# A residual with tokens on the partitions: output and down products with the activations stationary, norms tile by tile inside them, modulation on TensorE

## The chip, the cores and the metric

The kernel runs on one core of a Trainium2 chip. The metric is device time in microseconds (us) from the start to the end of one execution, as the median of several; the profile adds one execution with the time of every instruction. The engines are named as the profile names them: PE is TensorE (matmuls; PEld its weight loads), DVE is VectorE, ACT is ScalarE, POOL is GpSimd, and SP is the engine that issues nearly all DMAs. PE's clock has two levels, and "granted clock" 1.00 is the higher one, 2.4 GHz, 0.50 the lower.

## What is computed

Two layers of a diffusion backbone over 512 latent tokens and 256 context tokens, with 1024 features. Each sub-layer norms x, shifts and scales it, runs a mixer or the feed-forward part, norms the result, multiplies it by a gate and adds it to x. Shift, scale and gate come from a conditioning vector times a matrix of 1024 x 6144 per layer ("modulation"), and differ for latent and context tokens.

```python
for l in range(DEPTH):
    need_ctx = l < DEPTH - 1
    mod = jnp.split((silu_c @ ada_w[l] + ada_b[l])[:, None, :], 6, axis=-1)
    ...
    h = modulate(rms_norm(x, mix_pre_g[l]), mod[0], mod[1])
    ...
    x = x + mod[2] * rms_norm(y, mix_post_g[l])
    h = modulate(rms_norm(x, ffn_pre_g[l]), mod[3], mod[4])
    x = x + mod[5] * rms_norm(conv_ffn(h, ffn_w_in[l], ffn_conv_w[l], ffn_w_out[l]), ffn_post_g[l])
```

Layer 0's mixer is a convolution of width 31 beside a bidirectional mLSTM of four heads; layer 1's is a pooling group beside attention with six query heads. Both have one input and one output projection. `conv_ffn` is up product (gate and value, 2 x 2816 columns), a convolution of width 3 on the gate, silu, product and down product. In layer 1 only the latent tokens go on behind the mixer's keys and values.

## The kernel before

**Number format and products.** Every large product is three matmuls: both factors are split into a high part (`_hi`, the fp32r format) and a low part (`_lo`, the rest), and hi x hi, hi x lo and lo x hi are added in PSUM. `product` (matmul in L463) keeps 128 x 128 of weights stationary and moves 512 tokens and then 256 (only 512 in most of layer 1). A unit is 256 output features over all 1024 input features: 48 matmuls of 512 columns and 48 of 256.

**Weights** come in granules of 512 KB, two a unit. SP loads one to `raw` (two places), ACT makes `w_hi` (L855), DVE makes `w_lo` (L1247), and these have four places. The counters `low`, `high`, `unit_done` and `set_free` order all that: SP may load a granule when the one two before has its low part, and ACT may overwrite a `w_hi` when PE is done with its unit. PSUM `acc` has two sets, which the units take in turn; `set_free` gives one back. Each engine runs its instructions in the order in which its block writes them, and waits at a semaphore hold up all that stands behind them on that engine.

**Residual and norms.** The residual `xT` and the mixer's result `y` have features on the partitions, so a norm over features is a sum over partitions. It is a stage of its own between products: ACT squares 128 features of all tokens at a time (L880 for x, L891 for y), PE sums them by matmuls with a column of ones (`column_sums`, L498), DVE and ACT make the inverse root, PE spreads it over the partitions (`spread`, L510), and DVE and ACT do the residual (L1363), the normed and modulated value (L1344, ACT L903) and its low part (L1336). Matmuls without use (`keep_clock`, L518) run where PE would stand still in a norm. At the start x is loaded with tokens on the partitions, squared (L937) and transposed, and at the end `xT` is transposed back (L489), copied (L1239) and stored.

**Modulation.** The matrix comes in chunks of 256 columns, 1 MB each. DVE multiplies a chunk by the conditioning vectors and adds it up (L1259, L1266), PE sums that over the partitions inside a unit (L476), and ACT takes it (L869). The first eight chunks are shared by PE (L585) and DVE at the start, 8 to 11 lie in the even layer's input products, 12 to 19 in its output product, and the others in layer 0's feed-forward part.

**The order of stages.** Input products (`conv`, `gate`, `qkov`), the convolution's taps on DVE (L1474, `conv_done` after them, L1520), mLSTM, `out0`, two norms, then three groups of up and down products (`up00`, `down00`, ... `down02`, with 8, 8 and 6 tiles of 128 hidden features each), a norm of y and one of x, layer 1's `in1`, `kin`, `vin`, attention, `out1`, norms and `up10` to `down12`. The mLSTM goes through a list of items: "S" is a piece of scores (PE L699, ACT and DVE L1568 make `probs` of it), `weigh` multiplies probabilities by values (PE L672), "X" is the transposition of a head's result; the pieces of the convolution's norm (L641, L650) lie in the first head. The first half of out0's first unit stands in PE's queue ahead of the last head's transposition. DVE then merges a head with its gate, ACT and POOL (L1859) split it in `h_hi` and `h_lo`.

## Time and profile before

| | |
|---|---|
| median of 3 runs | 1904.1 us (1900.16 to 1906.55) |
| the profiled execution, its span | 1905.9 us |
| PE busy, weight loads | 1771.0 us (93%), 1501.2 us (79%) |
| DVE, ACT, POOL busy | 1149.3, 558.5 and 32.6 us |
| moved by DMA | 157.8 MB, 83 GB/s on average |

"Busy" counts all time in which an engine executes: matmuls that only keep the clock up count too. The chain of work that ended last tells, step by step back from the end, what each instruction waited for; the windows tell how busy each engine was in a stretch of the program.

### The profile page before, as it was taken

How to read it: one execution, taken by the hardware profiler on the slowest of the kernel's cores; microseconds unless marked ns; L12 is line 12 of the kernel's file. 1: busy time of each engine (PE TensorE's matmuls, PEld its weight loads, DVE VectorE, ACT ScalarE, POOL GpSimd, SP SyncE). 2: the span in 40 equal slices, each digit the busy share in tenths (PEclk: the TensorE clock that was granted, in tenths of full speed). 3: DMA queues.
4: the chain of work that ended last, by engine and by line, in shares of the span. 5: the costliest groups of instructions: out<-in, count | busy, mean ns of one | idle time of the engine just before them, and what ended most of it. 6: DMA issues, size and time to landing. Idle time of an engine off the chain costs nothing.

```text
span 1905.9 us, 25175 instructions
## 1 busy us (share of the span) xinstructions
PE 1771.0 (93%) x9614; PEld 1501.2 (79%) x9614; DVE 1149.3 (60%) x1899; ACT 558.5 (29%) x786; POOL 32.6 (2%) x68
## 2 busy tenths in 40 slices
PE   5899996777998999999999999999899999999997
PEld 3688875556897888888888888887587878888885
DVE  4787986455856776676755764542884555344344
ACT  3323222652123332123212222231232343222232
POOL 0000000220000000000000000000000000000000
PEclk9899996798987999999999999798999899999997
DMA  8232200012411334433332421040002033233321
GB/s 293 67 89 90 66 25 33 17 39 89 139 61 45 99 121 132 133 100 121 124 119 67 132 74 59 1 135 23 0 1 74 16 110 99 85 103 97 93 81 61
DMA packets 156405, 157.80 MB, mean 83 GB/s; under 512 B 9442, under 2 KB 153506, under 8 KB 156330
## 3 DMA queue, kind: packets, MB, share of 16 engines
q1 hardware_dynamic: 155760, 156.55, 25.8%
q8 instruction: 50, 0.82, 0.2%
q10 hardware_dynamic: 570, 0.22, 0.0%
q14 instruction: 25, 0.20, 0.0%
HBM read 154.63 MB, written 2.12 MB: 82 GB/s over the span
## 4 chain that ended last, share of the span: by engine, by line
PE 79%; DVE 13%; ACT 3%; DMA 2%; issue 2%; POOL 0%; ACTq 0%; SPq 0%; DVEq 0%
PE acc L463 60%; PE acc L518 3%; PE acc L498 3%; DVE conv_u L1474 3%; PE acc L829 2%; PE acc L476 2%; PE acc L808 2%; PE acc L672 1%; DVE tbuf L1344 1%; PE acc L489 1%; DVE h_lo L1336 1%; DVE ada_acc L1266 1%; DVE w_lo L1247 1%; PE acc L650 1%; PE acc L510 1%
## 5 line engine op out<-in xcount | busy, mean ns | idle before, releaser
L463 PE MATMUL acc<-h_hi,w_hi 128*128 128x512 f32 x1744 | 520.0, 357 | 18.4 <-DVE h_lo L1336 8.3
L463 PE MATMUL acc<-h_hi,w_lo 128*128 128x512 f32 x1744 | 516.9, 355 | 0.0
L463 PE MATMUL acc<-h_lo,w_hi 128*128 128x512 f32 x1744 | 515.3, 354 | 0.0
L463 PEld LDWEIGHTS acc<-h_hi,w_hi 128*128 128x128 f32 x1744 | 287.9, 191 | 69.4 <-issue 9.0
L463 PEld LDWEIGHTS acc<-h_lo,w_hi 128*128 128x128 f32 x1744 | 286.2, 191 | 47.1
L463 PEld LDWEIGHTS acc<-h_hi,w_lo 128*128 128x128 f32 x1744 | 286.2, 190 | 46.8
L1247 DVE TENSOR_TENSOR w_lo<-raw,w_hi 128x1024 fp32r<-128x1024 f32 x190 | 225.7, 1224 | 90.3 <-ACT w_hi L855 89.8
L855 ACT ACTIVATE w_hi<-raw 128x1024 fp32r<-128x1024 f32 x190 | 193.2, 1053 | 186.8 <-PE acc L463 97.5
L1266 DVE SCALAR_TENSOR_TENSOR ada_acc<-ada_w,cond,ada_acc 128x256 f32<-128x256 f32 x476 | 194.3, 479 | 1.6
L463 PE MATMUL acc<-hid_hi,w_hi 128*128 128x512 f32 (+1 forms) x528 | 160.1, 358 | 0.0
L463 PE MATMUL acc<-hid_lo,w_hi 128*128 128x512 f32 (+1 forms) x528 | 159.5, 356 | 0.0
L463 PE MATMUL acc<-hid_hi,w_lo 128*128 128x512 f32 (+1 forms) x528 | 159.4, 356 | 0.0
L1474 DVE SCALAR_TENSOR_TENSOR conv_u<-conv_u,dw_w 128x783 f32<-128x783 f32 x120 | 124.1, 1034 | 4.0
L869 ACT ACTIVATE mods<-acc,vec 128x2 f32 (+1 forms) x80 | 17.4, 262 | 363.3 <-PE acc L476 363.0
L1655 DVE TENSOR_SCALAR hid<-gpad,ffn_cw 128x512 f32 x66 | 25.2, 438 | 128.2 <-ACT gpad L1122 128.2
L463 PEld LDWEIGHTS acc<-hid_lo,w_hi 128*128 128x128 f32 x528 | 86.8, 188 | 15.5
L463 PEld LDWEIGHTS acc<-hid_hi,w_lo 128*128 128x128 f32 x528 | 86.7, 188 | 15.4
L463 PEld LDWEIGHTS acc<-hid_hi,w_hi 128*128 128x128 f32 x528 | 86.7, 188 | 15.0
L1247 DVE TENSOR_TENSOR y<-acc,y 128x1536 f32 (+5 forms) x18 | 24.0, 1342 | 89.9 <-PE acc L463 78.8
L1653 DVE SCALAR_TENSOR_TENSOR hid<-gpad,ffn_cw,hid 128x512 f32 (+1 forms) x132 | 77.6, 657 | 0.0
L518 PEld LDWEIGHTS acc<-ident,ones 128*128 128x128 f32 x528 | 70.4, 217 | 1.9 <-issue 1.0
L672 PEld LDWEIGHTS acc<-v_tok,probs 128*128 128x128 f32 x336 | 46.9, 220 | 31.2 <-DVE probs L1568 20.5
(225 smaller groups left out, 1697.9 us busy)
## 6 DMA issues: line engine op xcount, KB each, us to landing
raw<-in_ffn_w_in SPq DMA_DIRECT2D x88, 512.0 KB, 4.7
ada_w<-in_ada_w SPq DMA_DIRECT2D x80, 512.0 KB, 3.6
raw<-in_ffn_w_out SPq DMA_DIRECT2D x40, 512.0 KB, 4.5
raw<-in_even_w_in SPq DMA_DIRECT2D x24, 512.0 KB, 4.3
ada<-in_ada_w SPq DMA_DIRECT2D x8, 1024.0 KB, 12.2
raw<-in_odd_w_in SPq DMA_DIRECT2D x12, 512.0 KB, 3.6
raw<-in_even_w_out SPq DMA_DIRECT2D x8, 512.0 KB, 5.2
raw<-in_odd_w_out SPq DMA_DIRECT2D x8, 512.0 KB, 4.1
```

Source lines behind the costliest of these rows:

```text
L463: last = nc.tensor.matmul(acc[:, s, m, t0:t1], w[:, slot, kk, c], x[:, k, t0:t1], start=(k == 0 and q == 0), stop=(k == ktiles - 1 and q = ...
L476: last = nc.tensor.matmul(acc[:, s, 0, at_:at_ + 1], (ada_acc, second or ada_acc_b)[x][:, c, q * P:(q + 1) * P], ones[:, 0:1], start=True, ...
L498: last = nc.tensor.matmul(acc[:, s, 0, j:j + 1], src(j), ones[:, 0:1], start=(m == 0 and j == 0), stop=(m == len(sources) - 1 and j == til ...
L518: nc.tensor.matmul(acc[:, u % 2, 1, 512:512 + P], ones[:, :], ident[:, :], start=True, stop=True)
L672: last = nc.tensor.matmul(dst, probs[e % 4][:, t * P - t0:t * P - t0 + P], v_tok[:, ORDER[q], hd, :], start=(q, d, t) == FIRST_TOUCH[b], s ...
L808: last = nc.tensor.matmul(acc[:, 0, n % 2, t0:t1], inb[:, 2 + hd, i * P:(i + 1) * P], kT[:, hd // 3, t0:t1], start=True, stop=True)
L829: last = nc.tensor.matmul(acc[:, 1, 1, c:c + P], v1[:, j, (hd // 3) * HD:(hd // 3 + 1) * HD], pT[:, n % 2, j * P:(j + 1) * P], start=(j == ...
L855: nc.scalar.activation(w_hi[:, n % 4], raw[:, n % 2], ACT.Copy).then_inc(high, 1)
L1247: return nc.vector.tensor_tensor(out_, in0, in1, op)
L1266: ins = nc.vector.scalar_tensor_tensor(dst[:, c, :], w(k), scale, dst[:, c, :], ALU.mult, ALU.add)
L1474: ins = nc.vector.scalar_tensor_tensor(dst, src, tap, dst, ALU.mult, ALU.add)
L1653: ins = nc.vector.scalar_tensor_tensor(dst, src, c, dst, ALU.mult, ALU.add)
```

## The change

The residual `x` and `y` now have tokens on the partitions. `out0`, `out1` and the down products take 128 tokens of `h` or `hid` as the stationary operand and move 512 output columns of the weights (`token_products`, L637), in two halves of the output (`a` is 0 or 1), a half over all tiles of 128 tokens; a granule is 256 input features of 512 columns. The four products that a norm follows (`out0`, `down02`, `out1`, `down12`, "edges") do their second half tile by tile, and each tile's norm, gate, residual, next norm and transposition go on while PE does the other tiles: ACT squares with a running sum and takes roots, DVE updates x, PE transposes tile j-2 behind tile j (`turn`, L623), DVE modulates from PSUM, ACT makes `h_hi` and POOL `h_lo`. The first two units of what follows (up products or `in1`) run in segments of 256 tokens (`first_products`). The gates go as rows to DRAM and come back on all partitions. The norms' matmuls with ones, the fills and the transpositions at the end are gone, and x is stored as it is. Modulation: chunks 0 to 7 are matmuls with two moving columns at the start, 8 to 23 the same inside mLSTM (`ada_chunk`, L786, behind each "S" with q of 2 or more; the chunk is in the room of `raw`, one buffer of two halves), and layer 1's 24 chunks stay with DVE in `up00` and `up01`. The convolution's weights' low parts lie at other places on DVE, and out0 stands wholly behind the last head. The down products of layer 0 have 792 such matmuls, out0 has 288, out1 192, and layer 1's down products 528: 1800 in all.

```diff
+        def load_token(sp, name, w, first, k):
+            n, half = G[name] + k, TOK[name].half
+            a, g = divmod(k, half)
+            sp.wait_ge(low, n + 3)
+            sp.dma_start(raw[:, n % 2].rearrange("p (k a) c -> p k (a c)", k=2),
+                         w[:, first + 2 * g:first + 2 * g + 2, 512 * a:512 * a + 512]).then_inc(raw_full[n % 2], 16)
...
+            def load_ada_m(first, end):
+                for e in range(first, end):
+                    for half in range(2):
+                        if e:
+                            sp.wait_ge(adam_used, 2 * (e - 1) + half + 1)
+                        else:
+                            sp.wait_ge(low, G["out0"] + 8)
+                        sp.dma_start(ada_m[:, half], w_ada[0][:, 4 * half:4 * half + 4, (8 + e) * 256:(9 + e) * 256]
...
+                if h:
+                    load_ada_m(4 * h - 3, 4 * h + 1)
+            load_ada_m(13, 16)
+            def gate_rows(row, l, comp, streams):
+                for s in range(streams):
+                    sp.dma_start(g_dram[row + s].rearrange("(k p) -> p k", p=P), mods[:, l, comp, :, s],
+                                 allow_slow_non_contiguous=True).then_inc(gates_out, 16)
+            def gates_everywhere(row, dst, streams):
+                for s in range(streams):
+                    sp.dma_start(dst[:, s, :], g_dram[row + s].partition_broadcast(P)).then_inc(gates_in, 16)
+            sp.wait_ge(adam_used, 32)
+            load_token(sp, "out0", w_even_out, 0, 4)
+            load_token(sp, "out0", w_even_out, 0, 5)
+            sp.wait_ge(gates_set, 1)
+            gate_rows(0, 0, 2, 2)
+            gate_rows(2, 0, 5, 2)
+            sp.wait_ge(gates_out, 64)
+            gates_everywhere(0, gates[0], 2)
+            load_token(sp, "out0", w_even_out, 0, 6)
+            load_token(sp, "out0", w_even_out, 0, 7)
...
+        def first_products(pe, u, n, rhs, segs, ready, between, ada=None):
+            for e, (t0, t1) in enumerate(segs):
+                for x in range(2):
+                    s = (u + x) % 2
...
+                        if not x and not part:
+                            ready(e)
+                        for kk in range(4):
+                            k = 4 * part + kk
+                            for m in range(2):
+                                c = slice(m * P, (m + 1) * P)
+                                for q, (w, x_) in enumerate(((w_hi, rhs[0]), (w_hi, rhs[1]), (w_lo, rhs[0]))):
+                                    last = nc.tensor.matmul(acc[:, s, m, t0:t1], w[:, m_ % 4, kk, c], x_[:, k, t0:t1],
+                                                            start=(k == 0 and q == 0), stop=(k == KD - 1 and q == 2))
+                    if e == len(segs) - 1:
+                        if ada:
+                            last = ada_columns(pe, u + x, 0, ada[x])
+                    between(2 * e + x)
+        def turn(pe, name, j):
+            q = TOK[name].chain + j
+            pe.wait_ge(xn_ready, NT + q + 1)
+            if j >= 2:
+                pe.wait_ge(t_ready, KD + q - 1)
+            for k in range(KD):
+                last = nc.tensor.transpose(turned_bank(name, j, k), xn[j % 2][:, k * P:(k + 1) * P], ident[:, :])
+            last.then_inc(turned, 1)
...
+        def token_products(pe, name, lhs, ready):
+            def step(a, g, j):
+                m_ = n + a * half + g
+                for kk in range(2):
+                    k = 2 * g + kk
+                    for q, (w, x_) in enumerate(((w_hi, lhs[0]), (w_lo, lhs[0]), (w_hi, lhs[1]))):
+                        last = nc.tensor.matmul(tile_bank(name, a, j), x_[:, k, j * P:(j + 1) * P],
+                                                w[:, m_ % 4, 2 * kk:2 * kk + 2, :].rearrange("p a c -> p (a c)"),
+                                                start=(k == 0 and q == 0), stop=(k == 2 * half - 1 and q == 2))
+                return last
+            psum_free(pe, d)
+            for a in range(2):
+                if a and t.edge:
+                    for j in range(nt):
+                        if j >= 2:
+                            pe.wait_ge(tile_free, t.tiles + (j - 2 if j < 4 else nt + j - 2) + 1)
+                        for g in range(half):
+                            if not j:
+                                pe.wait_ge(low, n + half + g + 5)
+                            last = step(1, g, j)
+                            if j == nt - 1 and g < half - 1:
+                                last.then_inc(part_used, 1)
+                        last.then_inc(unit_done if j == nt - 1 else tile_full, 1)
+                        if name != "down12" and j >= 2:
+                            turn(pe, name, j - 2)
+                    continue
+                for g in range(half):
+                    pe.wait_ge(low, n + a * half + g + 5)
+                    ready(2 * g)
+                    ready(2 * g + 1)
+                    for j in range(nt):
+                        if not g and not a and j == 4 or not g and a and not j:
+                            psum_read(pe, d - 1)
+                        if not g and a and j >= 2:
+                            pe.wait_ge(tile_free, t.tiles + j - 1)
+                        last = step(a, g, j)
...
-            def norm_x(u, norm, tokens, diag_count):
-                psum_free(pe, u)
-                keep_clock(u, 70 * tokens // T)
-                column_sums(u, [lambda j, m=m: sq[:, m % 2, j * P:(j + 1) * P] for m in range(KD)], tokens // P,
-                            lambda m: pe.wait_ge(sq_ready, KD * norm + m + 1), sq_used)
-                keep_clock(u, 6)
-                spread(u + 1, diag, tokens, diag_count)
-                keep_clock(u + 1, 12)
...
+            def ada_chunk(e):
+                for q in range(2):
+                    c = 944 + 4 * e + 2 * q
+                    for k in range(KD):
+                        if not q and k % 4 == 0:
+                            pe.wait_ge(adam_full[k // 4], 16 * (e + 1))
+                        last = nc.tensor.matmul(acc[:, 0, 1, c:c + 2], ada_m[:, k // 4, k % 4, q * P:(q + 1) * P], cond[:, k, :],
+                                                start=False, stop=(k == KD - 1), skip_group_check=True)
+                        if q and k % 4 == 3:
+                            last.then_inc(adam_used, 1)
...
-                if z == len(ITEMS) - 1:
-                    assert U["out0"] % 2 == 0
-                    pe.wait_ge(sem("sums_read"), HEADS)
-                    product(pe, U["out0"], G["out0"], h, h_tiles(1), parts=(0,))
...
+                if kind == "S" and q >= 2:
+                    ada_chunk(chunk)
+                    chunk += 1
...
+            def x_squares(j, q):
+                nc.scalar.activation(xn[j % 2][:, :], x[:, j, :], ACT.Square, scale=1.0 / 32, accum_out=xsq[:, j:j + 1]
+                                     ).then_inc(sem("x_square"), 1)
+                act.wait_ge(sem("x_square"), q + 1)
+                nc.scalar.activation(xroot[:, 0, j:j + 1], xsq[:, j:j + 1], ACT.Sqrt, bias=eps[:, 0:1]).then_inc(x_root, 1)
+            def x_normed(j, q):
+                act.wait_ge(x_scale, q + 1)
+                nc.scalar.activation(xn[j % 2][:, :], x[:, j, :], ACT.Copy, scale=xroot[:, 1, j:j + 1]).then_inc(xn_ready, 1)
+            def tile_high(name, j):
+                act.wait_ge(t_ready, KD + TOK[name].chain + j + 1)
+                nc.scalar.activation(h_hi[:, :, j * P:(j + 1) * P], tb[j % 2][:, :, :], ACT.Copy).then_inc(t_high, 1)
...
+                    y_squares(name, 1, j)
+                    q = t.chain + j
+                    act.wait_ge(y_square, t.squares + nt + j + 1)
+                    nc.scalar.activation(yroot[:, 0, j:j + 1], ysq[:, j, 1:2], ACT.Sqrt, bias=ysq[:, j, 0:1]).then_inc(y_root, 1)
+                    if not on:
+                        continue
+                    if j >= 3:
+                        tile_high(name, j - 3)
+                    act.wait_ge(x_new, q + 1)
+                    if j >= 2:
+                        act.wait_ge(turned, q - 1)
+                    x_squares(j, NT + q)
+                    x_normed(j, NT + q)
...
+            def modulated(name, j, l, comp, tiles):
+                for k in tiles:
+                    last = nc.vector.tensor_scalar(tb[j % 2][:, k, :], turned_bank(name, j, k), mods[:, l, comp + 1, k, s_:s_ + 1],
+                                                   mods[:, l, comp, k, s_:s_ + 1], ALU.mult, ALU.add)
...
+                    summed(name, 2, 1, j)
+                    q = t.chain + j
+                    if on and j >= 2:
+                        modulated(name, j - 2, l, comp, range(0, 4))
+                    dve.wait_ge(y_root, q + 1)
+                    sd.done(nc.vector.reciprocal(yroot[:, 1, j:j + 1], yroot[:, 0, j:j + 1]))
+                    if not mixer:
+                        dve.wait_ge(y_gated, t.sums // 2 + j + 1)
+                    sd.wait()
+                    nc.vector.scalar_tensor_tensor(x[:, j, :], y[:, j, :], yroot[:, 1, j:j + 1], x[:, j, :], ALU.mult, ALU.add
+                                                   ).then_inc(x_new, 1)
+                    if not on:
+                        continue
+                    if j >= 2:
+                        modulated(name, j - 2, l, comp, range(4, 8))
+                    x_scales(j, NT + q)
+                for m in range(2, half) if on else ():
+                    take_low(n + half + m + 4)
+                for j in range(nt - 2, nt) if on else ():
+                    modulated(name, j, l, comp, range(8))
...
+                def tile_low(j):
+                    pool.wait_ge(t_high, KD + t.chain + j + 1)
+                    c = slice(j * P, (j + 1) * P)
+                    nc.gpsimd.tensor_tensor(h_lo[:, :, c], tb[j % 2][:, :, :], h_hi[:, :, c].bitcast(F32), ALU.subtract
+                                            ).then_inc(h_tile, 1)
+                for j in range(t.nt):
+                    if name[:3] != "out":
+                        pool.wait_ge(y_square, t.squares + t.nt + j + 1)
+                        nc.gpsimd.tensor_tensor(y[:, j, 512:1024], y[:, j, 512:1024],
+                                                gates[EDGES.index(name)][:, stream(j), 512:1024], ALU.mult).then_inc(y_gated, 1)
+                    if j >= 3 and name != "down12":
+                        tile_low(j - 3)
+                for j in range(t.nt - 3, t.nt) if name != "down12" else ():
+                    tile_low(j)
```

PE inside mLSTM, in the second half of a head, before (`qkov` is the scores' operand, `probs_72` and `probs_77` are probabilities, `h_tok` a head's result):

```order
L699 MATMUL acc<-qkov 128x512
L672 MATMUL acc<-v_tok,probs_72 128x129 x9
L672 MATMUL acc<-v_tok,probs_77 128x129 x2
L672 MATMUL acc<-v_tok,probs_72 128x129 x5
L489 MATMUL acc<-ident,h_tok 128x128 x6
L699 MATMUL acc<-qkov 128x512 x2
L672 MATMUL acc<-v_tok,probs_72 128x129 x3
L672 MATMUL acc<-v_tok,probs_77 128x129 x2
L699 MATMUL acc<-qkov 128x512
L672 MATMUL acc<-v_tok,probs_72 128x129 x5
L699 MATMUL acc<-qkov 128x512
```

and after, the same place (`ada_m` is a chunk of the modulation):

```order
L807 MATMUL acc<-qkov 128x512
L786 MATMUL acc<-cond,ada_m 128x2 x16
L774 MATMUL acc<-v_tok,probs_70 128x129 x9
L774 MATMUL acc<-v_tok,probs_75 128x129 x2
L774 MATMUL acc<-v_tok,probs_70 128x129 x5
L680 MATMUL acc<-ident,h_tok 128x128 x6
L807 MATMUL acc<-qkov 128x512
L786 MATMUL acc<-cond,ada_m 128x2 x16
L807 MATMUL acc<-qkov 128x512
L786 MATMUL acc<-cond,ada_m 128x2 x16
L774 MATMUL acc<-v_tok,probs_70 128x129 x3
L774 MATMUL acc<-v_tok,probs_75 128x129 x2
```

Behind each piece of scores there are 16 matmuls with two columns; between the first chunk of a head and the second 22 other matmuls and a score stand, between the second and the third one score.

PE between the last unit of out0 and the first up product, before (`ones` with `sumsq` and `sq` are the norms' sums, `ident,ones` fills):

```order
L476 MATMUL acc<-ones,ada_acc 128x1 x4
L476 MATMUL acc<-ones,ada_acc_b 128x1 x4
L518 MATMUL acc<-ident,ones 128x128 x6
L498 MATMUL acc<-ones,sumsq 128x1 x6
L498 MATMUL acc<-ones,sq 128x1 x12
L510 MATMUL acc<-diag,ones 128x512
L510 MATMUL acc<-diag,ones 128x256
L518 MATMUL acc<-ident,ones 128x128 x70
L498 MATMUL acc<-ones,sq 128x1 x48
L518 MATMUL acc<-ident,ones 128x128 x6
L510 MATMUL acc<-diag,ones 128x512
L510 MATMUL acc<-diag,ones 128x256
```

and after, inside out0's second half (`xn_87` is a normed tile of x):

```order
L637 MATMUL acc<-w_hi,h_hi 128x512
L637 MATMUL acc<-w_lo,h_hi 128x512
L637 MATMUL acc<-w_hi,h_lo 128x512
L623 MATMUL acc<-ident,xn_87 128x128 x8
L637 MATMUL acc<-w_hi,h_hi 128x512
L637 MATMUL acc<-w_lo,h_hi 128x512
L637 MATMUL acc<-w_hi,h_lo 128x512
```

The sums, spreads and fills are gone, and eight transposes of a tile lie between the products of two others.

ACT in the edge of out0, after (`junk` takes the squares of y, `xn` those of x and then the normed x, `tb_89` is a modulated tile); before, a norm stood alone in its queue:

```order
L1016 ACTIVATE junk_92,small<-acc 128x512
L1046 ACTIVATE small<-small 128x1
L1003 ACTIVATE h_hi<-tb_89 128x8x128
L990 ACTIVATE xn_88,small<-x 128x1024
L993 ACTIVATE small<-small 128x1
L998 ACTIVATE xn_88<-x,small 128x1024
L1016 ACTIVATE junk_91,small<-acc 128x512
L1046 ACTIVATE small<-small 128x1
L1003 ACTIVATE h_hi<-tb_90 128x8x128
```

A tile's squares, roots and normed x now stand in one queue with an older tile's `h_hi`, so the next tile's square waits for all of them.

## Rows read from the trace of the kernel before

**Rows 1.** The profile's page, first line and first part: busy us, share, instructions:

```profile
span 1905.9 us, 25175 instructions
PE 1771.0 (93%) x9614; PEld 1501.2 (79%) x9614; DVE 1149.3 (60%) x1899; ACT 558.5 (29%) x786; POOL 32.6 (2%) x68
```

**Rows 2.** The page's fourth part, shares of the chain that ended last:

```profile
PE 79%; DVE 13%; ACT 3%; DMA 2%; issue 2%; POOL 0%; ACTq 0%; SPq 0%; DVEq 0%
```

**Rows 3.** Windows by stage, one row each; columns as its first row says:

```profile
core 0: us, PE busy (x) PEld busy (x) DVE busy (x) ACT busy (x) POOL busy (x), PEclk, DMA share, GB/s
0.00:79.80 79.80, 51.53 (x268) 35.11 (x268) 41.08 (x96) 31.09 (x51) 3.83 (x7) 0.94 0.58 188
279.10:308.40 29.30, 9.36 (x54) 6.89 (x52) 28.30 (x30) 12.06 (x16) 1.03 (x2) 0.61 0.15 54
308.40:318.80 10.40, 10.38 (x49) 10.39 (x49) 1.71 (x4) 0.40 (x1) 0.29 (x1) 0.50 0.01 2
318.80:431.30 112.50, 87.12 (x471) 67.12 (x470) 52.71 (x123) 64.77 (x140) 25.60 (x57) 0.86 0.07 24
...
1293.10:1436.80 143.70, 129.59 (x773) 100.56 (x771) 95.93 (x167) 41.11 (x70) 0.00 (x0) 0.92 0.03 8
...
1878.90:1905.90 27.00, 14.52 (x70) 9.91 (x69) 12.56 (x22) 6.59 (x8) 0.00 (x0) 0.64 0.20 78
```

**Rows 4.** The chain in order of time: start us, us, engine, line, instructions:

```profile
98.55 1.68 PE acc L476 x16
...
541.99 17.08 PE acc L518 x140
559.07 17.53 PE acc L498 x96
...
631.99 16.76 PE acc L463 x96
...
1313.43 17.54 PE acc L783 x144
...
1526.86 352.03 PE acc L463 x1536
```

**Rows 5.** Groups by form: busy us, mean ns of one, idle us before, releaser:

```profile
L1266 DVE SCALAR_TENSOR_TENSOR ada_acc<-ada_w,cond,ada_acc 128x256 f32<-128x256 f32 x476 | 194.3, 479 | 1.6
L672 PE MATMUL acc<-v_tok,probs 128*128 128x129 f32 x336 | 49.9, 309 | 21.7 <-DVE probs L1568 21.7
L1363 DVE SCALAR_TENSOR_TENSOR xT<-y,mods,xT 128x512 f32<-128x512 f32 x32 | 23.6, 744 | 0.0
L1859 POOL TENSOR_TENSOR h_lo<-merged,h_hi 128x768 fp32r<-128x768 f32 x4 | 7.4, 1848 | 29.3 <-ACT h_hi L1063 29.3
L937 ACT ACTIVATE xsq_junk<-x_tok 128x1024 f32<-128x1024 f32 x6 | 6.4, 1061 | 0.1
```

**Rows 6.** Waits by pair: us in total, times, longest us:

```profile
PE acc L650 <- DVE mark L1520: 14.0, 1, 14.0
```

**Rows 7.** DMA issues: count, KB each, median us to landing:

```profile
ada_w<-in_ada_w SPq DMA_DIRECT2D x80, 512.0 KB, 3.6
...
raw<-in_even_w_in SPq DMA_DIRECT2D x8, 8.0 KB, 2.0
```

**Rows 8.** The timeline at several places: start us, us, engine, instruction:

```profile
93.84 2.35 DVE L1247 TENSOR_TENSOR w_lo<-raw,w_hi 128x1024 fp32r<-128x1024 f32 x2
...
444.94 0.82 PE L489 MATMUL acc<-ident,h_tok 128*128 128x128 f32 x6
...
447.78 1.87 POOL L1859 TENSOR_TENSOR h_lo<-merged,h_hi 128x768 fp32r<-128x768 f32 x1 [18.79 <-ACT h_hi L1063]
...
448.68 3.19 DVE L1247 TENSOR_TENSOR w_lo<-raw,w_hi 128x1024 fp32r<-128x1024 f32 x2 [1.61 <-ACT w_hi L855]
...
1900.47 1.94 ACT L1239 ACTIVATE o_tok<-acc 128x1024 f32<-128x1024 f32 x2 [1.18 <-PE acc L489]
```

1058 lines of the change are left out of this document (501 added, 557 removed).

## The prediction, made before the changed kernel ran

> **What bounds the kernel now.** I read the page first: of 1905.9 us TensorE (PE) is busy 93% [rows 1], and 79% of the chain that ended last is its work [rows 2]. But busy is not useful. The windows by stage [rows 3] show where PE works for nothing or waits: 28.3 us idle before the second unit of products, 20 us idle in the tail of the convolution (279.1 to 308.4, DVE busy 28.3 of 29.3), then column sums at a granted clock of 0.50 of full speed, and 12.5 us idle at the end. The chain in order of time [rows 4] shows what the norms between stages cost: in one norm of x, 17.1 us of matmuls L518 that only keep the clock up, and 17.5 us of column sums L498. Elsewhere PE runs product after product without a gap: a unit of 48 matmuls of 512 columns and 48 of 256 takes 16.76 us, and 1536 matmuls of 512 columns take 352.03, which is 0.2292 us each. With activations stationary and 256 columns moving (the value projection, L783), 144 take 17.54, 0.1218 each. So the form that the change introduces is there already, at half the width, and costs per column what the old one does.
>
> **Start to the first column sums of the convolution: -26.4.** Before, these sums end at 318.8 [rows 3]. The change takes the modulation of four chunks off DVE. A chunk costs it 14 instructions of 0.48 us [rows 5] and two smaller ones, some 7.4 us, so 30 in all. PE loses the three places where it folds them (1.68 each [rows 4], 5.0) and some 3.4 of waits for w_lo behind them. The first unit of products ends 4.7 earlier by my count (74 for 78.7): chunks 0 to 7 are matmuls with two columns, x is normed tile by tile (a square of 1024, 1.06 us, and a copy of the same size each), and after that POOL makes h_lo, 8 times 1.85 [rows 5]. That is 13.1 by the last unit of qkov. PE's wait of 14.0 for the convolution's last tile [rows 6] goes, since DVE has 30 us less in front of it; what is late next is PE itself. I add 0.7 for a copy that now stands behind the last unit. 13.1 + 14.0 - 0.7 = 26.4.
>
> **mLSTM: +38.5.** Sixteen chunks of 16 two-column matmuls go into PE's queue, four a head. The nearest row is L476, 16 in 1.68 us, so 27 for all at full clock. They also wait for data: one buffer of two halves, each freed by the last matmul that reads it, and a half of 512 KB lands in 3.6 us when alone [rows 7], 5.2 as the second of two by my estimate. The queue puts some 3.5 us of other work between chunks one and two of a head (22 matmuls of 128 or 129 columns at 0.14, as six transposes take 0.82 [rows 8], and a score), 0.3 between two and three and 1 between three and four, so some 10 us of waiting a head. Queued behind are the weighing of probabilities and the next scores, for which DVE and ACT wait. PE already waits 21.7 in this stage for DVE's probabilities [rows 5], 5 a head, and that covers part. I take 4 for the first head, where the convolution's norm leaves gaps, and 11.5 for each other one: 38.5. The bounds are 28 (only the matmuls) and 50 (nothing covered).
>
> **Last weighing to the end of the second up unit: -67.2.** Before, from 431.3 [rows 3] to 631.2, which is 0.8 before the row of the next unit starts [rows 4]: 199.9 us. After: out0 stands wholly behind the last head, whose norm, transposes, merge and modulation take 11.2 before PE may start, with 2.2 for a low clock; the first 512 output columns are 144 matmuls, 33.0. Then the second half, the turns and the first two up units. PE's own work there is 33.0, six times eight transposes at 1.05 a tile (a little under six's 0.82 by four thirds), and 288 matmuls of 256 columns at 0.1218, in all 74.4. The chain of a tile is longer than PE's 6.5: square 0.8, root, reciprocal, x update 1.29 (from 0.744 for 512 columns and 0.478 for 256), square 1.25, root, reciprocal, copy 1.05, with the semaphores 6.2. From the fourth tile on POOL's h_lo of 1024 columns (2.45, from 1.85 for 768) comes between, 8.4 to 8.8. Laid out tile by tile, the last tile is ready at 66 to 71, and the second unit ends at 83.8 to 88.6. I take 86.3. 11.2 + 2.2 + 33.0 + 86.3 = 132.7. The edge needs its gate rows: four DMAs of 1024 elements. The nearest row is 512 short runs in 2.0 us [rows 7], so 16 for the four, then two broadcasts; with 33 us until DVE wants them I charge nothing, and if that cover is gone each us late costs one.
>
> **To the end of kin: -40.5.** Before, 631.2 to 1293.1, 661.9. After: 20 up units at 16.75, 14 gaps of 0.78 for the modulation's fold, and 792 matmuls of the down products at 0.2292, 527.4 in all. The edge of down02, with y from SBUF, two multiplications more and three granules a half, ends 76 to 84 us after its first half, of which 24.8 is counted; 55.3. Then two units of 11.0 and one of 16.75. Sum 621.4.
>
> **Layer 1: -6.1.** Attention (143.7 us [rows 3]) is untouched. Before, out1 starts at 1436.8 and the second up unit ends at 1537.9, 11 after the last row of [rows 4] starts; 101.1. After: 22 + 73 by the same layout with four tiles. The rest of the FFN stays, its down products in the other form at the same price.
>
> **Tail: -17.6.** Before, 27.0 us stand behind the last product [rows 3]. After, the last tile's sum 0.7, square 0.8, gate on POOL 1.25, x update 1.29 and latencies, 5.9, and 3.5 for the last store (before, the last copy ends at 1902.4 [rows 8]). Small stalls that drop the clock: +3.
>
> The sum is -116.3, from 1905.9 to 1789.6. The profiled execution was 1.8 above the median of the runs shown, so 1788.
>
> **A rule weighed.** Two w_lo on DVE took 3.19 us where POOL's h_lo ran in front and into them, and 2.35 elsewhere [rows 8]; the first did not get going before POOL was done. I costed the edges half way between a DVE that waits so for every h_lo and one that never does. The Trainium skill ("SBUF — State Buffer", section "Who interferes with whom") has it that a VectorE instruction with two SBUF inputs and a GpSimd one exclude each other for their whole length, an exclusive lock on a shared port. By the rule the sum comes to 1795; with no lock anywhere, the start's 8 us included, to 1773.
>
> **The rivals.** (1) It goes better: no lock, and chunks that wait little (28 for 38.5): 25 less, 1763. For it speaks that DMA is 0.07 busy in mLSTM [rows 3]. 17%. (2) The waits for chunks put PE's clock down through mLSTM. The stage already has 0.86 with PE idle 25 us; at 0.50 the column sums took about twice their time. 30 more: 1818. 18%. (3) The tile chain is longer than laid out (periods of 11, or gate rows late), some 12 in each of three edges: 1825. Against it speaks that every operation in it has a row. 13%. (4) The other side: the down and output products. There are 1800 matmuls with tokens stationary and 512 weight columns moving; the trace shows that form only at 256 columns. If each took over 0.293 instead of 0.2292, 64 ns more, the 116 are gone, and at 0.31 the kernel is at 1935. Against it speaks L783 [rows 4]. 3%. That the norms' matmuls are not gone can't be: the order shows no L518.
>
> **How the numbers follow.** Forecast 49%, with its own range 1765 to 1805 (the bounds of mLSTM's 28 and 50, of the edges' lock). The range reaches into (1), (2) and (3): 1740 to 1832. A change of 0.3%, about 6 us, is what a measurement can tell; (1) to (3) and the forecast are all far below, so faster 0.96, slower 0.03 from (4), same 0.01.
>
> **What would show it.** In the changed profile: L637 at 0.229 us a matmul; two stretches of L786 with a wait for ada_m of 3 to 5 us in each head, and the last weighing near 443; in out0's edge a new x every 6 us, later every 8 to 9; the first up unit beginning some 45 us after the first half; no fills; 9 us from the last matmul to the end. The prediction is wrong if PE waits over 15 us a head, if the granted clock in mLSTM is near 0.5, or if L637 is over 0.25.

## The result, and the profile after

The changed kernel takes 1941.05 us (median of 4, 1934.49 to 1943.12) against 1903.55 for the kernel before beside it. The ratio of the runs is 1.0181, 95% interval 1.0159 to 1.0204: slower by 1.6 to 2.0%, clear of the noise though not clearly over 2%, where the prediction had 1788 and gave "slower" 0.03. Its profiled execution spans 1940.8 us, 34.9 more than before.

The page of the kernel after, first and fourth part:

```profile
span 1940.8 us, 23097 instructions
PE 1771.4 (91%) x9170; PEld 1512.9 (78%) x9170; DVE 962.0 (50%) x1488; ACT 564.3 (29%) x817; POOL 100.0 (5%) x102
...
PE 74%; DVE 11%; ACT 5%; issue 4%; DMA 3%; POOL 1%; ACTq 0%; DVEq 0%; POOLq 0%; SPq 0%
PE acc L584 33%; PE acc L637 18%; PE acc L608 3%; PE acc L786 3%; PE acc L774 3%; PE acc L708 3%; DVE ada_acc L1370 2%; DVE w_lo L1351 2%; PE acc L680 2%; DMA ada_w<-in_ada_w 2%; PE acc L948 2%; DVE x L1493 2%; PE acc L927 2%; PE acc L807 1%; ACT xn L990 1%
```

PE is as busy as before to half a microsecond (1771.0 in [rows 1]), although fills and column sums are gone: something as large has come in. New in the chain are L708 and L786, the chunks of the modulation, and DVE's sums of layer 1 with their loads. The windows by stage say where (columns as in [rows 3]):

```profile
42.65:97.06 54.41, 54.41 (x258) 54.41 (x256) 11.12 (x21) 6.76 (x8) 11.72 (x6) 1.00 0.19 58
333.84:529.90 196.06, 179.44 (x983) 158.44 (x982) 53.00 (x123) 64.99 (x140) 25.80 (x57) 0.72 0.30 93
541.20:582.00 40.80, 40.76 (x169) 33.54 (x170) 9.05 (x14) 8.14 (x17) 1.83 (x1) 0.94 0.48 75
582.00:660.10 78.10, 70.94 (x464) 65.36 (x463) 47.51 (x101) 35.59 (x59) 14.63 (x6) 0.96 0.18 56
660.10:788.70 128.60, 114.29 (x633) 99.68 (x634) 89.79 (x175) 37.62 (x44) 0.00 (x0) 0.91 0.34 106
856.30:1031.10 174.80, 154.53 (x833) 134.65 (x832) 110.19 (x198) 36.72 (x58) 0.00 (x0) 0.91 0.43 135
1227.00:1303.30 76.30, 61.87 (x351) 54.67 (x350) 49.04 (x90) 36.21 (x60) 22.02 (x12) 0.87 0.10 30
1342.10:1492.40 150.30, 133.59 (x771) 104.33 (x771) 98.12 (x169) 42.16 (x70) 0.00 (x0) 0.89 0.05 15
```

Laid beside the prediction's own stages (the differences are after less before, in us; the 3 us that the prediction adds for small stalls belong to no row):

| stage | before | after | foretold | measured |
|---|---|---|---|---|
| start to the end of the first column sums of the convolution | 318.8 | 333.8 | -26.4 | +15.0 |
| mLSTM, to the last weighing | 112.5 | 196.1 | +38.5 | +83.6 |
| to the end of the second up unit | 199.9 | 130.2 | -67.2 | -69.7 |
| to the end of kin | 661.9 | 682.0 | -40.5 | +20.1 |
| attention | 143.7 | 150.3 | 0 | +6.6 |
| out1 to the start of the third up unit | 101.1 | 99.5 | -6.1 | -1.6 |
| the rest of layer 1's products | 341.0 | 340.9 | 0 | -0.1 |
| behind the last product | 27.0 | 8.0 | -17.6 | -19.0 |

The residual's part came as foretold: norms, edges, tail. Three stages miss by 41, 45 and 61 us, 147 together, of an error of 151 (1940.8 for 1789.6). In all three the modulation is computed, in the first two by two-column matmuls on PE, in the third by DVE, whose sums PE folds (adds up over the partitions, L566) inside a unit. The chain in order of time shows what a chunk costs there:

```profile
42.65 54.41 PE acc L708 x256
97.06 214.65 PE acc L584 x1200
...
398.09 3.47 PE acc L786 x32
...
460.16 4.92 DMA ada_m<-in_ada_w
465.12 5.28 PE acc L786 x24
...
583.60 1.30 DVE x L1493
589.19 1.30 DVE x L1493
596.05 1.30 DVE x L1493
602.90 2.73 DVE x L1493
...
611.19 2.72 DVE x L1493
...
671.92 1.87 PE acc L566 x8
673.79 19.40 PE acc L584 x96
```

A chunk is 16 matmuls in the program and 32 records in the trace: at best 3.47 us, 0.108 a record. At the start a record takes 0.2125 (54.41 / 256), and behind a wait for data 0.22 (5.28 / 24). The rows "DMA ada_m" are the loads from issue to landing; PE itself stands idle for less of it, here 1.80 and 0.35 us, since a score and eight records of the next chunk go on beside the load. I had taken "16 in 1.68" of [rows 4] for one chunk. The order printed ahead of the prediction has that place as 4 + 4 matmuls, so 16 records were 8 matmuls already.

### The profile page after: what moved, and what is told of

Same layout as the page of the kernel before. It is cut to its first block, busy times and chain, and to the rows that moved or that the text cites. A ratio compares the mean times of both kernels' runs of the same rounds, so it can differ in the third digit from the quotient of the medians.

```text
span 1940.8 us, 23097 instructions
## 1 busy us (share of the span) xinstructions
PE 1771.4 (91%) x9170; PEld 1512.9 (78%) x9170; DVE 962.0 (50%) x1488; ACT 564.3 (29%) x817; POOL 100.0 (5%) x102
## 4 chain that ended last, share of the span: by engine, by line
PE 74%; DVE 11%; ACT 5%; issue 4%; DMA 3%; POOL 1%; ACTq 0%; DVEq 0%; POOLq 0%; SPq 0%
PE acc L584 33%; PE acc L637 18%; PE acc L608 3%; PE acc L786 3%; PE acc L774 3%; PE acc L708 3%; DVE ada_acc L1370 2%; DVE w_lo L1351 2%; PE acc L680 2%; DMA ada_w<-in_ada_w 2%; PE acc L948 2%; DVE x L1493 2%; PE acc L927 2%; PE acc L807 1%; ACT xn L990 1%
## 5 line engine op out<-in xcount | busy, mean ns | idle before, releaser
L584 PE MATMUL acc<-h_hi,w_hi 128*128 128x512 f32 (+1 forms) x1424 | 420.4, 357 | 1.7 <-DVE w_lo L1351 1.7
L584 PE MATMUL acc<-h_lo,w_hi 128*128 128x512 f32 (+1 forms) x1424 | 420.6, 357 | 0.0
L584 PE MATMUL acc<-h_hi,w_lo 128*128 128x512 f32 (+1 forms) x1424 | 418.9, 356 | 0.0
L584 PEld LDWEIGHTS acc<-h_hi,w_hi 128*128 128x128 f32 x1424 | 235.3, 193 | 40.8 <-DVE w_lo L1351 1.9
L637 PE MATMUL acc<-w_hi,hid_hi 128*128 128x512 f32 x440 | 176.1, 400 | 0.0
L637 PE MATMUL acc<-w_lo,hid_hi 128*128 128x512 f32 x440 | 175.5, 399 | 0.0
L637 PE MATMUL acc<-w_hi,hid_lo 128*128 128x512 f32 x440 | 175.2, 398 | 0.0
L608 PE MATMUL acc<-h_hi,w_hi 128*128 128x256 f32 x224 | 69.7, 311 | 39.1 <-POOL h_lo L1962 25.8
L1370 DVE SCALAR_TENSOR_TENSOR ada_acc<-ada_w,cond,ada_acc 128x256 f32<-128x256 f32 x224 | 102.2, 493 | 5.8 <-DMA ada_w<-in_ada_w 1.6
L637 PEld LDWEIGHTS acc<-w_hi,hid_lo 128*128 128x128 f32 x440 | 83.6, 190 | 20.4
L637 PEld LDWEIGHTS acc<-w_hi,hid_hi 128*128 128x128 f32 x440 | 83.7, 190 | 20.2
L637 PEld LDWEIGHTS acc<-w_lo,hid_hi 128*128 128x128 f32 x440 | 83.6, 190 | 20.1
L786 PEld LDWEIGHTS acc<-cond,ada_m 128*128 128x128 f32 x512 | 76.7, 237 | 20.2 <-DMA ada_m<-in_ada_w 12.2
L786 PE MATMUL acc<-cond,ada_m 128*128 128x2 f32 x512 | 75.6, 281 | 7.5 <-DMA ada_m<-in_ada_w 7.3
L608 PEld LDWEIGHTS acc<-h_hi,w_hi 128*128 128x128 f32 x224 | 48.1, 215 | 40.8 <-issue 27.6
```

Of the source, the lines that this page charges most:

```text
L584: last = nc.tensor.matmul(acc[:, s, m, t0:t1], w[:, slot, kk, c], x_[:, k, t0:t1], start=(k == 0 and q == 0), stop=(k == KD - 1 and q == 2))
L608: last = nc.tensor.matmul(acc[:, s, m, t0:t1], w[:, m_ % 4, kk, c], x_[:, k, t0:t1], start=(k == 0 and q == 0), stop=(k == KD - 1 and q == 2))
L637: last = nc.tensor.matmul(tile_bank(name, a, j), x_[:, k, j * P:(j + 1) * P], w[:, m_ % 4, 2 * kk:2 * kk + 2, :].rearrange("p a c -> p (a ...
L786: last = nc.tensor.matmul(acc[:, 0, 1, c:c + 2], ada_m[:, k // 4, k % 4, q * P:(q + 1) * P], cond[:, k, :], start=False, stop=(k == KD - 1 ...
L1370: ins = nc.vector.scalar_tensor_tensor(dst[:, slot, :], w(k), scale, dst[:, slot, :], ALU.mult, ALU.add)
```

## The experiments

All are edits of the changed kernel. One profiled execution each unless said otherwise; times are spans of that execution and stand against its 1940.8.

One span against another says less than it seems to, because stages without an edit differ between executions too. "Start" is from the first chunk to the first product, up00 is from the end of the second up unit to down00, in us:

| kernel | start | mLSTM | up00 | up01 | attention | span |
|---|---|---|---|---|---|---|
| the changed kernel | 54.4 | 196.1 | 128.6 | 174.8 | 150.4 | 1940.8 |
| 1, no modulation of layer 1 | 52.2 | 204.3 | 108.8 | 133.1 | 150.0 | 1879.8 |
| 2, one chunk | 51.7 | 193.1 | 129.1 | 173.9 | 146.5 | 1925.1 |
| 3, no chunks | 51.3 | 111.9 | 125.0 | 174.8 | 145.0 | 1844.2 |
| 4, fills | 78.6 | 195.9 | 128.8 | 175.4 | 145.0 | 1961.5 |
| 5, rows at the start | 35.6 | 206.4 | 126.2 | 174.8 | 148.5 | 1925.1 |
| 6, 64 columns | 54.4 | 178.1 | 128.9 | 175.4 | 145.0 | 1920.0 |
| 7, second buffer | 51.4 | 185.6 | 126.7 | 173.8 | 145.0 | 1918.7 |
| 8, buffer and 64 columns | 54.4 | 150.3 | 124.9 | 174.3 | 150.0 | 1885.8 |
| 9, early table load | 51.8 | 199.6 | 120.3 | 174.5 | 147.5 | 1926.7 |
| 10, neither modulation | 54.4 | 113.5 | 108.4 | 135.6 | 145.0 | 1787.3 |
| 11, spread | 51.3 | 199.3 | 120.0 | 156.9 | 149.0 | 1910.5 |
| 12, all together | 35.6 | 154.5 | 121.1 | 148.6 | 148.5 | 1844.7 |

Where nothing was edited, the start takes 51.3 to 54.4, mLSTM 195.9 to 206.4 and attention 145.0 to 150.4. So what an edit is worth is read in its own stage, and a difference of a few us in a span is not its work.

**1. No modulation of layer 1.** The loads, DVE's sums, PE's folds and ACT's reading are out; constants stand for the values.

```diff
-                    chunks = () if l else ((1,), (1, 2), ())[g]
+                    chunks = ()
...
-                    ada = 0 if l else (28, 24, 0)[g]
+                    ada = 0
```

> The changed kernel with layer 1's modulation left out of up00 and up01 (no chunk loads, no sums on DVE, no folds on PE, no reading of them on ACT; constants stand for the values). Theory A: PE waits in these two stages for DVE's sums, and the clock falls behind each wait. Then the 14 units there, 309 us in the two stages, go to about 16.8 each, 235, and the span to about 1866. Rival: the new places of the weights' low and high parts hold PE up, sums or not: less than 25 us are won and the span stays over 1915.

Measured 1879.8: 61.0 less. The chain shows no stop between units: six in 104.61 us in up00 (17.4 each, the first at a low clock), eight in 133.13 in up01 (16.6 each), with the down products of 67.47 between:

```profile
667.58 104.61 PE acc L583 x576
772.19 67.47 PE acc L636 x288
839.66 133.13 PE acc L583 x768
```

The two stages are 61.5 us shorter (19.8 and 41.7); theory A had more, 1866, in part because its 309 us count 6 of the second up unit. PE's waits for the sums in the changed kernel are 34.6 us of that, and the rest is the clock behind them and the folds:

```profile
PE acc L566 <- DVE ada_acc L1370: 34.6, 11, 11.8
```

Theory A holds for nearly all of it; the new places of the low parts hold up next to nothing in these stages.

**2. One chunk loaded in mLSTM, used sixteen times.** **3. No chunks in mLSTM.**

```diff
-                            pe.wait_ge(adam_full[k // 4], 16 * (e + 1))
+                            pe.wait_ge(adam_full[k // 4], 16)
...
-                if h:
-                    load_ada_m(4 * h - 3, 4 * h + 1)
-            load_ada_m(13, 16)
```

```diff
-                if kind == "S" and q >= 2:
-                    ada_chunk(chunk)
-                    chunk += 1
```

> The changed kernel with one chunk of layer 0's modulation loaded in mLSTM and used 16 times: the same matmuls on PE, no wait for the other fifteen loads (so 15 chunks hold wrong values). Theory A: waits of some 12 us in all and a low clock behind them cost about 30 us, so mLSTM goes from 196 to about 166 and the span to 1911. Rival: the matmuls themselves are the price, at two records each, and at most 8 us are won.

> The changed kernel without any of the 16 chunks in mLSTM: no matmuls, no loads, the modulation of components 2 to 5 is the bias alone. By theory A mLSTM goes back to about 112, 84 less than 196, of which 30 are what the kernel with one chunk wins and 54 the 512 records at 0.107; span 1857. Rival: other changes in mLSTM (out0's first part taken out, other places on the queues) cost some of it, and mLSTM stays over 125.

Measured 1925.1 and 1844.2. Without chunks mLSTM is as before (111.9 us for 112.5), so the chunks are the whole of its loss, 84.2 us. The span is 96.6 shorter: 3.9 lie ahead of mLSTM and 8.5 behind it, where nothing was edited; by the table 3.1 of them are the start, 3.6 up00 and 5.4 attention, and at least the first and the last of these vary as much between other executions. With no load to wait for, the span is 15.7 us shorter, but mLSTM only 2.9 (193.1 for 196.1, granted clock 0.70), where theory A had 30 and the rival at most 8; the rest lies in stages without an edit. Two windows of the kernel with one chunk show why:

```profile
350.00:360.00 10.00, 10.00 (x43) 8.97 (x42) 2.20 (x5) 3.79 (x5) 0.58 (x2) 0.50 0.00 0
412.00:429.00 17.00, 17.00 (x76) 15.97 (x74) 1.77 (x4) 1.12 (x2) 0.58 (x2) 0.50 0.00 0
```

And its chain, inside the second:

```profile
412.11 6.62 PE acc L783 x32
```

PE is busy without a gap for 17 us, waits for nothing, and stands at a granted clock of 0.50, the 1.2 GHz level; a chunk takes 6.62 us instead of 3.47. So theory A, in which the clock falls behind the waits, does not reach: from 405 to 411 the granted clock is 1.00 and from 411 on 0.50, with PE busy throughout, in a stretch that is mostly two-column matmuls.

**4. Fills between the chunk matmuls at the start.** Four matmuls of 128 columns ahead of each group of eight.

```diff
+                    for _ in range(4):
+                        nc.tensor.matmul(acc[:, u % 2, 1, 576:576 + P], ones[:, :], ident[:, :], start=True, stop=True)
```

> The changed kernel with four matmuls of 128 columns without use ahead of each group of eight two-column matmuls at the start, 64 in all. Theory: the 128 two-column matmuls there (256 records) take 0.2125 us a record, twice what they take in mLSTM, since so little moves through the array that PE runs at half pace. With the fills the records go to 0.107, 27 us, the fills cost 17, and the start is some 10 us shorter (span 1931). Rival: the pace comes from the weight loads or from waiting for the chunks; then the fills only add their 17 us or more, span 1958.

Measured 1961.5. The fills cost 1.92 us a group (8 records of 0.24). The chunks' records begin near full pace (0.116) and are at 0.20 within 9 us, without a gap between; the clock of the stretch is low, so the pace is the clock's, but this mixture does not hold it up:

```profile
44.28 1.86 PE acc L710 x16
...
51.42 3.21 PE acc L710 x16
```

```profile
42.57:121.18 78.61, 78.61 (x386) 78.61 (x384) 11.13 (x21) 6.76 (x8) 11.73 (x6) 0.53 0.13 41
```

The theory's remedy failed, and the span is what the rival had (1958). But a pace set by the weight loads or by waiting would not be full first and half later over the same instructions; run 5 tests the form itself.

**5. The start's chunks in the form of before:** two columns of vectors stationary, 256 of the chunk moving.

```diff
-                        last = nc.tensor.matmul(acc[:, u % 2, o // 4, c:c + 2], ada_0[:, o % 6, k, q * P:(q + 1) * P], cond[:, k, :],
...
+                    last = nc.tensor.matmul(acc[0:2, (u + 1) % 2, o % 2, 0:256], cond[:, k, :], ada_0[:, o % 6, k, :],
...
```

> The changed kernel with the first eight chunks in the form of before: the conditioning vectors are stationary, 256 columns of the chunk move, a row of 256 is copied by ACT and turned by two transposes. Theory: with 256 columns moving PE gets to its full pace, 16 records a chunk at 0.221 as before, so the eight take about 31 us for 54 and the span is about 1916; the products behind start at full pace too. Rival: the pace at the start is half whatever PE does there (it comes out of the gaps between the transposes); then a chunk takes over 7 us and the span stays over 1938.

Measured 1925.1, 15.7 less. The chain:

```profile
44.04 7.07 PE acc L717 x32
51.32 3.54 PE acc L717 x16
55.08 3.54 PE acc L717 x16
...
74.67 3.47 issue
78.14 36.06 PE acc L585 x192
```

A chunk takes 3.54, and the first product starts at 78.14 for 97.06: 18.9 us won in place. PE comes out of the same gaps between transposes, so the rival falls: it reaches full pace there (0.221 a record from the first chunk on), and the two-column form loses it. The span won less than the 25 expected: PE now waits 3.47 us for the first h_lo, the products behind start at half clock again, and mLSTM, which has no edit here, took 10 us more in this execution (206.4).

**6. Chunk matmuls of mLSTM with 64 columns moving** (of the identity: these modulations hold other values).

```diff
-                        last = nc.tensor.matmul(acc[:, 0, 1, c:c + 2], ada_m[:, k // 4, k % 4, q * P:(q + 1) * P], cond[:, k, :],
+                        last = nc.tensor.matmul(acc[:, 0, 1, 944:1008], ada_m[:, k // 4, k % 4, q * P:(q + 1) * P], ident[:, 0:64],
...
```

> The changed kernel with the chunk matmuls of mLSTM moving 64 columns of the identity instead of two of the conditioning vectors (so these modulations hold other values); the same weights are loaded, the same waits stand. Theory: a record is set by its weight load at 0.107 and two moving columns let the clock fall, 64 keep it up; then the records of 0.207 go to about 0.11 and mLSTM is 25 to 35 us shorter than 196. Rival: what moves does not matter for the clock here; mLSTM stays within 5 us of 196, or grows by 512 times what 62 columns more cost.

Measured 1920.0, 20.8 less, 18 of them in mLSTM (178.05 for 196.06, granted clock 0.85 for 0.72), where the theory had 25 to 35. The same chain now reads:

```profile
437.06 3.52 PE acc L786 x32
443.50 1.38 PE acc L774 x10
446.40 3.53 PE acc L786 x32
449.95 4.76 DMA ada_m<-in_ada_w
454.75 5.38 PE acc L786 x24
```

32 records take 3.52 with 64 columns, 3.47 with two: more columns cost nothing, and keep the pace. What stood behind the half pace comes to light, more waiting for the next chunk: the load takes 4.76, PE is idle for 1.83 and 0.84 of it, and behind these waits the clock is low once more (5.38 for 24).

**7. A second buffer for the chunks**, in the room of two granules of out0 that are then split after the last head. **8. The second buffer and 64 columns**, with every modulation computed: the vectors stand in a row of zeros and the window over it is shifted.

```diff
-                            sp.wait_ge(adam_used, 2 * (e - 1) + half + 1)
+                            sp.wait_ge(adam_used, 2 * (e - 2) + half + 1)
```

```diff
-                    c = 944 + 4 * e + 2 * q
+                    c = 14 - 4 * (e % 4) - 2 * q
...
+                        last = nc.tensor.matmul(acc[:, 0, 1, 944:1008], ada_m[e % 2][:, k // 4, k % 4, q * P:(q + 1) * P],
+                                                cz[:, k, c:c + 64],
```

> The changed kernel with a second buffer for the chunks of mLSTM, in the room of the split weights of out0's third and fourth granule, which are now made after the last head. Every chunk but one can be there when PE comes to it. Theory A (the half pace comes from the two-column matmuls themselves): the waits go and the records of 0.207 stay, so only 10 to 16 us are won, as with one chunk used 16 times; span 1925 to 1931. Rival: the clock falls because of the waits; then 30 us or more, span under 1911.

> The kernel with the second buffer, and 64 moving columns in each chunk matmul: the conditioning vectors stand in a row of zeros, the window over it is shifted so that each chunk's sums come out in their own columns, and DVE takes them once a head. Theory A: neither waits nor half pace are left, mLSTM falls from 196 to 112 + 16 x 3.5 = 168 or a little under it, span about 1912. If the two causes do not add up (waits that only come to light at full pace), over 175 and span over 1919.

Measured 1918.7 and 1885.8. The spans are 22.1 and 55.0 shorter. In mLSTM itself the buffer alone wins 10.5 (185.6), which is theory A's 10 to 16 and far from the rival's 30; the other 11.6 lie in stages without an edit, 5.4 of them in attention. Both together win 45.8 there (150.3), more than the 28 that I gave them and more than 10.5 + 18.0. The mLSTM windows of run 8, then of run 3 (no chunks at all):

```profile
330.73:481.00 150.27, 137.35 (x982) 121.90 (x982) 53.44 (x126) 64.77 (x140) 25.81 (x57) 0.94 0.36 116
```

```profile
329.94:441.85 111.91, 86.61 (x470) 67.00 (x470) 52.69 (x123) 64.77 (x140) 25.55 (x57) 0.86 0.07 24
```

Sixteen chunks at 3.52 are 56.3 us of PE, and the stage grows by 38.4: PE's idle time in it falls from 25.3 to 12.9, and at 0.94 the stage's other matmuls are faster too. So of the 84 us that the chunks cost in the changed kernel, 38 are their work, net, and 46 were the clock and the waits for data; taking away one of the two alone gives back 10.5 or 18.0, since each hid a part of the other.

**9. One activation of one column ahead of ACT's wait** in the loop over up products.

```diff
+                        nc.scalar.activation(small[:, 69:70], eps[:, 0:1], ACT.Identity, bias=eps[:, 0:1])
                         psum_full(act, u, i)
```

> The changed kernel with one activation of one column at the head of ACT's loop over the up products, ahead of its wait for PE, so that the table load of 1.28 us stands in ACT's idle time and not between the end of a unit and the copy of the gate. Theory: in up00 that load makes DVE's second sum end 0.9 us after PE's unit, and the half clock behind the wait does the rest; without it the six units from 654 us on go from 22.4 to about 17.6 each, 28 us, and up01, whose sums wait for their chunks, wins less than 10. Span 1905 to 1913. Rival: DVE is late by more than the load; less than 8 us in all.

The timeline of the changed kernel shows the place that this is about:

```profile
694.19 1.28 ACT L981 ACT_TABLE_LOAD   x1 [14.42 <-PE acc L566]
...
695.79 1.52 ACT L1258 ACTIVATE gpad<-acc 128x1024 f32<-128x1024 f32 x2
...
705.86 5.75 DVE L1370 SCALAR_TENSOR_TENSOR ada_acc<-ada_w,cond,ada_acc 128x256 f32<-128x256 f32 x14
...
711.67 1.05 PE L566 MATMUL acc<-ones,ada_acc 128*128 128x1 f32 x8 [0.93 <-DVE ada_acc L1370]
...
713.86 0.85 PE L584 MATMUL acc<-h_hi,w_hi 128*128 128x512 f32 x2
```

PE ends a unit; ACT waited 14.42 us for it and only then loads its table (1.28 us); then come the gate's copy, DVE's taps and low parts, and the sum, which ends 0.93 us after PE wants it. Behind that wait two records take 0.85 for 0.51. The Trainium skill ("ScalarE: Activation LUTs", section "What ACT_TABLE_LOAD costs") gives 1283 ns, which the trace has, and a drain of about 1380 ns beside it, of which this place shows nothing: the next activation starts at 695.49.

In the kernel before, the load stood behind hid_hi, while ACT had time (timeline):

```profile
671.12 1.28 ACT L855 ACT_TABLE_LOAD   x1
```

Measured 1926.7, 14.1 less, of which 8.3 lie in up00 (120.3 for 128.6); the start and attention, without an edit, are shorter by 2.6 and 2.9, and mLSTM is longer by 3.5. The theory had 28 in up00. Its 22.4 a unit was a misreading: 134.7 us from 654 on hold the last 6 of the second up unit and 13.6 until the next unit starts, and the six units came every 19.2. Now they come every 17.5 to 17.9:

```profile
689.41 16.75 PE acc L584 x96
706.95 17.06 PE acc L584 x96
724.80 16.75 PE acc L584 x96
```

So a wait of 0.93 us cost some 3 a pair of units (pairs of 38.9, 38.1 and 37.8 us before, 35.4 after). The stop of over 10 us ahead of the first pair, in which DVE is late from the edge, is still there, and up01 is not better (174.5 us), as expected.

**10. No chunks in mLSTM and no modulation of layer 1.**

> The changed kernel without the chunks of mLSTM and without layer 1's modulation (both as in the runs that left out one of them). If the costs add up, 1880 and 1844 give 1940.8 - 61.0 - 96.6 = 1783. This is the change of the residual and of the norms alone, with the start as it is. If the two share waits it is up to 10 us more.

Measured 1787.3. The two costs add up to within 4 us (1783). This is the change without 40 of its 48 chunks; that it lies near my 1788 is chance, since that number held 38.5 for mLSTM's chunks and 10.9 for layer 1's folds, and too little for the start.

**11. Layer 1's chunks spread** over up01 (three a pair) and up02, with run 9's edit.

```diff
-                    ada = None if l else (((0, 2, True), (1, 2, True)), ((9, 4, False), (11, 4, False)), (None, None))[g]
+                    ada = None if l else (((0, 2, True), (1, 2, True)), ((9, 3, 2), (10, 3, 1)), ((20, 2, 1), (21, 2, 1)))[g]
...
```

> The changed kernel with layer 1's modulation in thinner layers: three chunks for a pair of units in up01 instead of four, the others in up02 (two of them are computed twice, to fill its loop), and the table load of ACT ahead of its wait. Theory: four chunks for a pair need 4 x (4.5 landing + 1.9 for the half that can't overlap), 26 us, with DVE's 14 of other work more than a pair's 35; three are 19 + 14 and fit. Then up01 goes from 174.8 to about 142 and up02 from 101.8 to about 105; span 1926.7 - 30 = 1897. Rival: in-order work on DVE (sums behind taps and low parts) stalls PE with three as well: up01 stays over 158.

Measured 1910.5, 16.2 less than with run 9's edit alone, where I had 30. up01 takes 156.9 us: better than 174.8, and not the 142 that I summed from DVE's work. The chain has the rival's mark, a load that the sum waits for and a low clock behind it:

```profile
893.32 4.77 DMA ada_w<-in_ada_w
900.30 1.87 PE acc L568 x8
902.17 19.11 PE acc L586 x96
```

In up02, one chunk a unit, six units take 103.1 us, 17.2 each. How up01 should be ordered for none at all I did not try.

**12. All together** (runs 5, 8, 9 and 11), three rounds.

> All together: the start's chunks in row form, the second buffer and 64 columns in mLSTM, the table load ahead and layer 1's chunks spread. If the gains add up: 1940.8 - 15.7 (start) - 29 (mLSTM) - 44 (up stages) = 1852, some 50 under the kernel before. Rival: gains overlap, or a new wait takes 20 us or more: over 1872.

Measured 1847.28 us (median of 4, 1840.36 to 1852.4) against 1904.1; the ratio is 0.9696, interval 0.966 to 0.9733: 3% faster than the kernel before. Stage by stage it keeps what the single runs won: 18.8 at the start, 41.5 in mLSTM, 7.5 in up00 and 26.2 in up01, 94 of the 96.1 us in the profiled execution (1844.7). I had expected 1852, with 29 for mLSTM. Nothing of the computation is left out.

## Why the prediction was wrong

- **"mLSTM: +38.5" was the step that failed most clearly,** in its term "the nearest row is L476, 16 in 1.68 us, so 27 for all at full clock". The records are two a matmul: 16 chunks are 55.5 us at full clock (16 x 3.47), 28 more. The clock was put at nothing, and slower matmuls, the chunks' own and the others, cost 37 more (PE is busy 92.3 us longer than before, 179.44 for 87.12, of which 55.5 are the chunks at full pace). The third term was too large: I took some 10 us of waiting a head, 11.5 in all net of what it covers, and PE's idle time in the stage fell by 8.8 (from 25.4 to 16.6); it stands 7.3 us in all before chunk matmuls for their data. One reason is the same misreading: the work between two chunks of a head, which I had at 3.5 us, is 5.8 at full pace (run 6, 440.6 to 446.4), since the weighing's matmuls too are two records each. 28 + 37 - 20 is the miss of 45. Rival (2) had the clock, but as a result of the waits and at 30 us more; run 2 (no waits for loads, 2.9 us won) and runs 6 and 8 put it on the two-column matmuls first.
- **"Start: -26.4"** rests on the same price. Eight chunks, some 13 us by it, take 54.4, and half clock makes half of that; in the old form they take 30 (run 5). That is the whole miss of 41: the other terms err by some 4 us either way. The stage from the last unit of qkov to the sums is 22.1 us for 39.7, with the wait of [rows 6] gone, 4.3 better than worked out. (The unit that I had ending at 78.7 before ends at 77.9.)
- **"To the end of kin: -40.5"** failed at "20 up units at 16.75, 14 gaps of 0.78". I counted the folds, not what PE has to wait for before a fold: that layer 1's sums, spread over all of layer 0's products before, now lie in 14 units. PE waits 34.6 us for them, and run 1 prices the whole at 61.5 us in up00 and up01, which is the miss (61); run 9 gives 8 of them to the table load. It stood in the diff, and I had the rows: a chunk is 7.4 us on DVE, a load 3.6 or more. down02's edge, in the same stage, came out at 76.3 for 80.
- **The step "last weighing to the second up unit"** was right, to 2.5 us in all, and in part by terms that cancel: 11.3 ahead of out0 (11.2), 40.8 for the first half (35.2 with the clock), 78.1 for the edge (86.3). **Layer 1 and the tail** are right to 5 and 1.4 us. Matmuls with tokens stationary cost 67.60 us for 288, 0.2347 each: rival (4) is out.
- **None of the three signs of being wrong came up:** PE's waits for chunks are under 2 us a head for 15, the clock in mLSTM is 0.72 and not near 0.5, L637 is at 0.2347 for 0.25. They watched the waits and the products, not the price of a chunk or the place of layer 1's sums.
- **The rule weighed.** The x update takes 1.30 us in out0's first three tiles and 2.73 once POOL makes h_lo beside it, and new x came 5.6, 6.9, 6.9 and 8.3 us apart, as laid out (the rows of L1493 in the chain above). POOL's own 1024 columns take 2.417. That is the exclusion which the Trainium skill states ("SBUF — State Buffer", "Who interferes with whom"); the trace agrees, and no run removed it. The trace does not say which part of the length is the port and which the order of the two queues.
- **Attention** is 6.6 us longer in the changed kernel's profile, without an edit in its own loop. Over the thirteen profiled executions of the changed kernel and its edits it takes 145.0 to 150.4, against 143.7 in the one of the kernel before, so most of the 6.6 can be this execution's own; 1.3 to 6.7 us are what the executions show, and why it varies is open. With "faster" at 0.96 I had put my doubts into the new residual and the waits for chunks, and none into the price of a chunk or into layer 1's sums.

## What to carry to other kernels

Count matmuls by the instruction before pricing them by a row: the number of records in a group need not be that of instructions, and the order of the program tells. When work moves to an engine "with room", price it at its new place: here 16 chunks on PE cost 84 us as written and 38 with a second buffer and 64 moving columns, and the same sums on DVE cost PE a fold of 0.78 us a unit where they lay thin and 61 us in two stages where they lay thick. A short stall on PE can cost about three times its length through the clock (0.93 us, some 3 a pair), so a 1.28 us table load in front of a copy is worth moving. And compare runs by stage: here stages without an edit moved a span by as much as 10 us.

## What was not expected of the hardware

- PE at 100% busy can run at half clock: 17 us of two-column matmuls and weighing at 0.50, without a gap. 64 moving columns instead of two take the same time a record (3.52 for 3.47 a chunk) and keep the higher clock. The Trainium skill ("TensorE: Matmul & The Clock Gate", section "HAM oscillation — how this bites in real kernels") advises padding thin products, for kernels that wait for DMA; here padding pays without such waits as well (150.3 for 185.6 us in mLSTM, run 8 against run 7). Four fills of 128 columns between groups of eight, at the start, did not do the same (run 4), and why is open.
- At the start the column PEclk reads 1.00 for 42.65 to 97.06 while records take twice their time; in run 3 the same matmuls at the same pace (49 records in the 10 us from 50 on, for 48) stand at 0.50, behind 3.5 us at 1.00 in which 30 records went through. Where pace and granted clock differ, the pace of a known row is the safer reading.
- Four DMAs of 1024 single elements each were 21 us from the first issue until the broadcast could go (541.15 to 562.6), 5.4 each; nobody waited for them.
